# Turning half of each sample's key pages in 32x32 blocks on VectorE, the other half on TensorE, in one core's hybrid decoder layer

## The reference, cut to what matters

```python
q, k, v, g_a, qi, wi, ki, u, g_b = project(hs, ln_g[layer], w_in[layer])
o_a = sample_attention(q, k, v, qi, wi, ki, cache_k[layer], cache_v[layer],
                       cache_idx_k[layer], page_table, rel_bias)
o_b = multiscale_pool(u_full, past - POOL_STATE, POOL_STATE, w_pool[layer], pool_scale[layer])
hs = merge(hs, o_a, g_a, o_b, g_b, w_out[layer])      # x + [o_a*silu(g_a); o_b*silu(g_b)] @ w_out
...
# sparse_attend: logits of each query against the selected keys of its group
logits = jnp.einsum('btgrd,btkgd->btgrk', qg, k_sel, preferred_element_type=F32) * (D ** -0.5)
p = jax.nn.softmax(logits + bias, axis=-1)
o = jnp.einsum('btgrk,btkgd->btgrd', p.astype(v_sel.dtype), v_sel)
```

## Time and profile before

| | us |
|---|---|
| median of three runs | 2083.04 (2082.86 to 2083.18) |
| span of the profiled execution | 2081.8 |
| TensorE busy | 2067.9 (99%) |
| VectorE busy | 1288.9 (62%) |
| ScalarE busy | 735.1 (35%) |
| GpSimd busy | 406.3 (20%) |
| the segment "ga" in the trace | about 1315 to 1615 |

### The profile page before, as it was taken

The page is one execution under the profiler, slowest core; times in us unless marked ns, Lnnn a source line. Parts: engine busy times, 40 slices in busy tenths (PEclk is TensorE's granted clock), DMA queues, the critical chain, the costliest instruction groups (busy, mean ns, idle before and its releaser), DMA issues. The chain is left out here.

```text
span 2081.8 us, 38884 instructions
## 1 busy us (share of the span) xinstructions
PE 2067.9 (99%) x14191; PEld 1973.7 (95%) x14191; DVE 1288.9 (62%) x1747; ACT 735.1 (35%) x917; POOL 406.3 (20%) x574
## 2 busy tenths in 40 slices
PE   9999999999999999999999999999999999999998
PEld 7888888999999999999999999999999999999998
DVE  5545545578687445666776767565565866555664
ACT  6433333322222333333333323333334433333333
POOL 1100000021210010235642103222222511111100
PEclk9999999999999999999999999999999999999999
DMA  8777777755554565665666657878877855555554
GB/s 234 208 220 214 222 211 203 212 167 159 157 160 140 179 192 171 176 195 174 195 201 201 178 153 231 242 245 260 248 248 246 258 170 169 164 164 165 157 167 147
DMA packets 341330, 406.03 MB, mean 195 GB/s; under 512 B 20332, under 2 KB 316204, under 8 KB 341000
## 3 DMA queue, kind: packets, MB, share of 16 engines
q1 hardware_dynamic: 293704, 291.75, 47.6%
q0 software_dynamic: 29968, 94.61, 14.7%
q10 hardware_dynamic: 17584, 18.70, 2.7%
HBM read 377.68 MB, written 31.45 MB: 197 GB/s over the span
## 5 line engine op out<-in xcount | busy, mean ns | idle before, releaser
L246 DVE TENSOR_TENSOR lo<-raw,hi 128x1024 fp32r<-128x1024 f32 x542 | 694.5, 1285 | 566.6 <-ACT hi L241 565.2
L270 PE MATMUL main<-XX,hi 128*128 128x320 f32 x3264 | 1030.1, 316 | 0.2 <-DVE XX L1655 0.2
L272 PE MATMUL main<-XX,lo 128*128 128x320 f32 x3264 | 1009.5, 309 | 0.0
L271 PE MATMUL main<-XX,hi 128*128 128x320 f32 x3264 | 1009.0, 309 | 0.0
L241 ACT ACTIVATE hi<-raw 128x1024 fp32r<-128x1024 f32 x542 | 569.8, 1057 | 854.7 <-PE main L272 540.6
L270 PEld LDWEIGHTS main<-XX,hi 128*128 128x128 f32 x3264 | 613.2, 188 | 9.0 <-issue 5.0
L271 PEld LDWEIGHTS main<-XX,hi 128*128 128x128 f32 x3264 | 613.3, 188 | 2.3
L272 PEld LDWEIGHTS main<-XX,lo 128*128 128x128 f32 x3264 | 612.7, 188 | 0.0
L257 PE MATMUL main<-XX,hi 128*128 128x512 f32 x1024 | 355.9, 392 | 0.0
L258 PE MATMUL main<-XX,lo 128*128 128x256 f32 x1024 | 287.0, 280 | 0.0
L257 PEld LDWEIGHTS main<-XX,hi 128*128 128x128 f32 x1024 | 191.6, 187 | 42.4 <-issue 0.2
(11 more groups left out here) (304 smaller groups left out, 1544.8 us busy)
## 6 DMA issues: line engine op xcount, KB each, us to landing
raw<-w_in SPq DMA_DIRECT2D x416, 512.0 KB, 3.9
raw<-w_out SPq DMA_DIRECT2D x128, 512.0 KB, 3.7
deck<-cache_k POOLq DMA_DIRECT2D x64, 256.0 KB, 4.4
projT<-stg ACTq DMA_DIRECT2D x35, 320.0 KB, 2.9
keep<-cache_v POOLq DMA_DIRECT2D x40, 256.0 KB, 3.4
deck<-cache_v POOLq DMA_DIRECT2D x24, 256.0 KB, 3.6
deck<-maskD POOLq DMA_DIRECT2D x8, 516.0 KB, 5.6
ipg<-cache_idx_k POOLq DMA_DIRECT2D x64, 64.0 KB, 3.1
```

The costliest lines, as they stand in the source:

```text
L246: nc.vector.tensor_tensor(low, raw[:, slot, :, 0:width], high.bitcast(F32), ALU.subtract).then_inc(lo_ready, 1)
L270: nc.tensor.matmul(sums, wh, XH[:, k, :], start=first, stop=False)
L271: nc.tensor.matmul(sums, wh, XL[:, k, :], start=False, stop=False)
L272: mm = nc.tensor.matmul(sums, wl, XH[:, k, :], start=False, stop=last)
```

## The change

TensorE transposes only pages 0 to 3 of a sample, two in s = 1 and two in s = 2, and ScalarE copies all four. Pages 4 to 7 are turned by VectorE straight from `kpg` to `KTs`: 16 instructions a sample, each turning the 32x32 blocks of one row quarter and one column quarter in all four pages and four groups at once. They are spread by two tables. For a sample with u = 0 (after the first) 4 stand in slot 14 and 1 in slot 15 of the quad before, then 4, 4 and 3 in slots 0, 1 and 2. For u = 1 there are 4 in slot 6, 5 in slot 7, none in slot 8, 3 in slot 9 and 4 in slot 10. Sample 0 has 8 in slot 1 and 8 in slot 2. The first turn waits for the sample's pages (e_kw) and for the scores of the sample before (e_s); the last one raises e_kd, for which the scores in s = 3 and the next load of pages 4 to 7 wait. GpSimd loads pages 4 to 7 first, after e_kd, and then pages 0 to 3, after e_kt. VectorE's loop over the quads has its first one written out apart.

```diff
+        e_kw, e_kd = sem("e_kw"), sem("e_kd")
...
+            PE_PAGES = PAGES // 2
...
                 if s in (1, 2):
-                    for p in range(4 * s - 4, 4 * s):
+                    for p in range(2 * s - 2, 2 * s):
                         if p == 0:
-                            pe.wait_ge(e_k, b * (16 * PAGES) + 16 * PAGES)
+                            pe.wait_ge(e_k, b * (16 * PE_PAGES) + 16 * PE_PAGES)
...
-                        if p >= 4:
-                            pe.wait_ge((e_kcA, e_kcD)[p % 2], b * (PAGES // 2) + (p - 4) // 2 + 1)
                         for g in range(G):
-                            tr = nc.tensor.transpose(sbank[p % 4][:, g * P:(g + 1) * P], kpg[:, p, g * P:(g + 1) * P], ident[:])
+                            tr = nc.tensor.transpose(sbank[p][:, g * P:(g + 1) * P], kpg[:, p, g * P:(g + 1) * P], ident[:])
                         tr.then_inc(e_kt, 1)
                 if s == 3:
-                    pe.wait_ge(e_kcA, b * (PAGES // 2) + PAGES // 2)
-                    pe.wait_ge(e_kcD, b * (PAGES // 2) + PAGES // 2)
+                    pe.wait_ge(e_kcA, b * PE_PAGES + PE_PAGES)
+                    pe.wait_ge(e_kd, b + 1)
                     pe.wait_ge(e_kn, b * 2 + 2)
...
-            def turned_keys(eng, copy, s, b, even, done):
-
+            def keys_free(eng, b):
                 eng.wait_ge(e_s, b)
                 eng.wait_ge(w_pe, 4 * NG)
                 eng.wait_ge(ut_out, 16 * NG * (NB_S + 1))
-                for p in range(4 * s - 4 + (0 if even else 1), 4 * s, 2):
-                    eng.wait_ge(e_kt, b * PAGES + (p + 1))
-                    copy(KTs[:, :, p * P:(p + 1) * P], sbank[p % 4].rearrange("p (g n) -> p g n", g=G)).then_inc(done, 1)
+
+            def turned_pages(dve, b, start, count):
+
+                if not count:
+                    return
+                if start == 0:
+                    dve.wait_ge(e_kw, b * (16 * (PAGES - PE_PAGES)) + 16 * (PAGES - PE_PAGES))
+                    keys_free(dve, b)
+                    alone(dve)
+                for i in range(start, start + count):
+                    a, j = i // 4, i % 4
+                    src = kpg[32 * a:32 * a + 32, PE_PAGES:PAGES, :].rearrange("p n (g k) -> p n g k", g=G)
+                    dst = KTs[32 * j:32 * j + 32, :, PE_PAGES * P:PAST].rearrange("p g (n k) -> p n g k", k=P)
+                    ins = nc.vector.transpose(dst[:, :, :, 32 * a:32 * a + 32], src[:, :, :, 32 * j:32 * j + 32])
+                if start + count == 16:
+                    ins.then_inc(e_kd, 1)
+
+            TURNS = ({-2: 4, -1: 1, 0: 4, 1: 4, 2: 3}, {-2: 4, -1: 5, 0: 0, 1: 3, 2: 4})
+            FIRST_TURNS = {1: 8, 2: 8}
...
                 if s in (1, 2):
-                    turned_keys(act, lambda o, i: nc.scalar.activation(o, i, ACT.Copy), s, b, True, e_kcA)
+                    keys_free(act, b)
+                    for p in range(2 * s - 2, 2 * s):
+                        act.wait_ge(e_kt, b * PE_PAGES + (p + 1))
+                        nc.scalar.activation(KTs[:, :, p * P:(p + 1) * P], sbank[p].rearrange("p (g n) -> p g n", g=G),
+                                             ACT.Copy).then_inc(e_kcA, 1)
...
-            def dve_weave(dve, q, j):
+            def dve_weave(dve, q, j, first=False, last=False):
                 u, s = j // 8, j % 8
                 b = q * BQ + u
-                if s in (1, 2):
-                    turned_keys(dve, nc.vector.tensor_copy, s, b, False, e_kcD)
+                if s in (6, 7) and not (last and u):
+                    turns = TURNS[1 - u]
+                    turned_pages(dve, q * BQ + (u + 1), 0 if s == 6 else turns[-2], turns[s - 8])
+                if s in (0, 1, 2):
+                    turns = FIRST_TURNS if first and u == 0 else TURNS[u]
+                    turned_pages(dve, b, sum(n for at_, n in turns.items() if at_ < s), turns[s] if s in turns else 0)
...
-                load_pages(pool, 0, "cache_k", keys, e_k)
+                load_pages(pool, 0, "cache_k", keys, e_k, 0, PE_PAGES)
+                load_pages(pool, 0, "cache_k", keys, e_kw, PE_PAGES)
...
                 with pool.Fori(1, NB_S) as b:
-                    pool.wait_ge(e_kt, b * PAGES)
+                    pool.wait_ge(e_kd, b)
                     alone(pool)
-                    load_pages(pool, b, "cache_k", keys, e_k)
+                    load_pages(pool, b, "cache_k", keys, e_kw, PE_PAGES)
+                    pool.wait_ge(e_kt, b * PE_PAGES)
+                    alone(pool)
+                    load_pages(pool, b, "cache_k", keys, e_k, 0, PE_PAGES)
```

More of the change, by code:

```diff
@@ L422, in hybrid_layer @@
         gated_a, exped_a = sem("gated_a"), sem("exped_a")
-        (e_in, e_rel, e_k, e_v, e_mask, e_masked, e_vnew, e_kt, e_kcA, e_kcD, e_kn, e_s, e_lg, e_mx, e_exp, e_ri, e_pt,
+        (e_in, e_rel, e_k, e_v, e_mask, e_masked, e_vnew, e_kt, e_kcA, e_kn, e_s, e_lg, e_mx, e_exp, e_ri, e_pt,
          e_ptA, e_pv, e_on, e_ot, e_o) = (sem(n) for n in (
-             "e_in", "e_rel", "e_k", "e_v", "e_mask", "e_masked", "e_vnew", "e_kt", "e_kcA", "e_kcD", "e_kn", "e_s", "e_lg",
+             "e_in", "e_rel", "e_k", "e_v", "e_mask", "e_masked", "e_vnew", "e_kt", "e_kcA", "e_kn", "e_s", "e_lg",
              "e_mx", "e_exp", "e_ri", "e_pt", "e_ptA", "e_pv", "e_on", "e_ot", "e_o"))
@@ L1656, in dve_mix, with then_mix @@
                                         ALU.subtract).then_inc(f_lo, 1)
-            def then_mix(weave, mix):
+            def then_mix(weave, mix, **kw):
                 def last_weave(eng, q, j):
-                    weave(eng, q, j)
+                    weave(eng, q, j, **kw)
                     if j in (13, 14):
@@ L1814, in on_gpsimd @@
                     pool.wait_ge(stored[half], 16 * segs["ga"][4])
-                pool.wait_ge(e_kt, NB_S * PAGES)
+                pool.wait_ge(e_kt, NB_S * PE_PAGES)
+                pool.wait_ge(e_kd, NB_S)
                 pool.wait_ge(e_kn, NB_S * 2)
@@ L1870, in on_vector @@
             def on_vector(dve):
-                with dve.Fori(0, NQ - 1) as q:
+                dve_quad(dve, "ga", 0, lambda eng, q, j: dve_weave(eng, q, j, first=True), gate=gate)
+                with dve.Fori(1, NQ - 1) as q:
                     dve_quad(dve, "ga", q, dve_weave, gate=gate)
-                dve_quad(dve, "ga", NQ - 1, then_mix(dve_weave, dve_mix), gate=gate, open_end=True)
+                dve_quad(dve, "ga", NQ - 1, then_mix(dve_weave, dve_mix, last=True), gate=gate, open_end=True)
                 dve_quad(dve, "out", 0, mix_weave(dve_mix, dve_gating), turned=turn_part, first=True)
```

## The result

The changed kernel takes 2117.61 us (median of four runs, 2117.39 to 2118.09) against 2083.09 for the kernel before (median of four as well): a ratio of 1.0166, 95% interval 1.0154 to 1.0178. It is 34.5 us slower. The profiled execution spans 2116.1 us, 34.3 more than before.

What follows compares the result with a forecast made beforehand. TensorE, busy 99% of the span, was taken as the bound. Span 2081.8 - 14.0 (transposes) + 33.6 (stalls) + 3.5 (clock) = 2104.9 us; with the runs' median 1.2 above the span, 2106 us, range 2098 to 2119.

Steps and rivals of the forecast that it cites:

- rival 1: Clock behind TensorE's stalls: falls each time, four chunks at half speed, 14 us in place of 3.5, 2116 us; chance 0.24.
- Gain on TensorE: TensorE's queue before the scores: 16 fewer transposes, 1.75 us less for each of 8 samples, 14.0 us in all.
- Price of a turn: VectorE's 32x512 turn: 0.70 us with the step between instructions, extended from rows of 128, 192 and 256 elements.
- rival 2: VectorE's turns are cheap: at 0.50 us stalls cancel the gain (2083), below it faster; chance 0.10 shared with another rival.
- Stalls: TensorE ahead of the scores: 8.4 us at sample 0, three of 5.0, four of 2.55, together 33.6 us.
- Clock: TensorE's clock behind stalls: one slow chunk, 3.5 us, for the longest stall, nothing for the others; bounds 0 to 14.
- Edits at nothing: Split key loads, turns in slots 6 and 14, late splits and output-stage loads: all covered by slack, costing nothing.
- margin of the loads: Late key pages land some 9 us after the scores begin, VectorE asks later than 11 us: 2 us of margin.
- None hides another: The eight stalls add up, since each chain starts anew at a half quad's evacuation, which waits for TensorE.

Runs made afterwards that it cites:

- filled run: Changed kernel with idle matmuls (56, 34 or 17) put in TensorE's queue ahead of its wait for the turns; 2107.26 us, ratio 1.0116.
- five pages: Changed kernel with sample 0 on TensorE and ScalarE, other turns in VectorE's idle places, and VectorE turning five of eight pages in samples 1 to 7; 2098.69 us.
- sample 0 taken back: Changed kernel, but TensorE transposes all eight pages of sample 0, ScalarE copies them and VectorE turns none; 2108.98 us, ratio 1.0121.

## Why the prediction came out as it did

The direction and the mechanism held: TensorE's queue was the bound, 14.0 us left it, and VectorE's queue behind each evacuation held up the scores eight times (at sample 0 behind the stage's first splits). The measured time, 2117.6 us, lies in the range but at rival 1's 2116, not at the forecast's 2106; the loss was 34.5 us where 23 were forecast. It lies outside the 2098 to 2111 that the prediction gave its own mechanism, and is in the range only because that took in rival 1. That rival 1 comes within 2 us is in part luck: it had 33.6 us of stalls and 14 of clock, the runs show 37.2 and 10.8, and the two misses cancel.

- **Gain on TensorE**, 14.0 us: with 15 of 16 turns left out 13.4 were measured.
- **Price of a turn**, 0.70 us: 702 ns in the row, and (1416.11 - 1413.25) / 4 = 0.715 from turn to turn. The slope through three sizes held, and rival 2 needed 0.50. The prices of the Trainium skill's section on the three transpose paths ("VectorE: DVE Perf Modes"), which are for bf16, did not carry over: VectorE takes 0.70 us for as many elements as a 128x128 tile has, TensorE's transposes step by 0.109 us.
- **Stalls**, 33.6 us: measured 37.2 (8.80, 16.4 at samples 2, 4 and 6, 11.9 at the odd ones). The terms were 8.4, 15.0 and 10.2. What was left out is the step between unlike instructions: from a split to the turn behind it are 1413.25 - 1411.99 = 1.26 us, where the earlier trace rows have (1402.91 - 1400.63) / 2 = 1.14 a split. For samples 2, 4 and 6 three such places and 0.015 more for each of 11 turns make 3 x 0.12 + 0.17 = 0.5 us a sample.
- **Clock**, 3.5 us: this is the step that failed. The prediction charged one chunk for the longest stall and nothing for the rest. The clock fell after all four long stalls and after one of 2.91 us, and cost 10.8 us by the traces and 10.35 by the filled run. The mis-sizing was in how often, not in how much: per stall it was 1.6 to 2.7 us, under the 3.5 charged. For the short stalls the nearest row, 1.5 us at full clock, was what it went by, and three of four bore it out. The three stalls of 5 us were put at nothing without a reason, although nothing between 1.5 and 5 us had been seen; they cost 2.7, 2.5 and 2.4 us, 7.6 of the 10.8. The Trainium skill, "TensorE: Matmul & The Clock Gate", part 1, puts such stalls at risk, and here the trace agrees with it: 0.50 granted behind 5.56 us.
- Sum by the measured terms: - 14.0 + 37.2 + 10.8 = 34.0, against 34.3 between the spans.
- **Edits at nothing** held in the changed kernel: no wait for a key page, none at the normalisation, and VectorE still waits 1.84 us for TensorE at the evacuation in slot 15. The margin of the loads was larger than the 2 us put on it. The last late page of sample 2 is issued at 1386.10, pages land 3.7 us after issue in this stretch, and VectorE's first turn stands at 1396.39:

```profile
1386.10 0.54 POOL L1794 DMA_DIRECT2D deck<-cache_k  x1 [0.69 <-issue]
...
1396.39 2.84 DVE L1471 STREAM_TRANSPOSE deck<-deck 32x512 f32<-32x512 f32 x4
```

That makes some 6 us: VectorE asks 15.1 us after the scores of 1381.28, not 11. The runs with turns in slot 5, and five pages most of all, used the margin up.

- "None hides another" held: without sample 0's stall the others stayed at 28.0 us, where they had 28.4.

## What to carry to other kernels

Mean load says whether work fits on an engine at all; where it fits is read from the instruction that others wait for, back to the last point at which that queue was itself held. Work behind such a point (here the evacuation and the gate) adds to the chain one for one, while the same instructions in places where the engine waits anyway are nearly free (here until the loads of their pages came too late): moving the turns of seven samples took 36 us off, by a table of small numbers. And a stall of TensorE by 3.67 us or more cost more than its length each time here, since what came behind it ran at half clock; so first remove the stalls, and then price the rest.

## What the runs showed of the hardware

**The clock behind a stall.** By the lengths of the scores in the traces (1.97 us at full clock): no stall up to 1.96 us slowed them; of nine of 2.91 to 3.01 us four did (changed kernel one of four, sample 0 taken back two of four, five pages its only one); all twelve of 3.67 to 8.80 us did. So a stall near 3 us goes either way, even between samples of one execution. In the changed kernel each of the five drops cost 1.6 to 2.7 us. These are the idle times in the brackets of the traces, and all of them stand in a stream that otherwise keeps TensorE busy.

**Turns on VectorE in fp32.** 314, 378, 436, 702 and 836 ns for 128, 192, 256, 512 and 640 elements on 32 partitions: 1.04 ns per element from 256 on. The first two sizes read another tile (`main`, a PSUM bank) than the others, so the slope below 256 compares unlike operands. The Trainium skill, "Vector Engine (DVE) Microarchitecture Reference", section 3.8, has the reorder array sustain one element per cycle and lane; a constant price per element is what these rows show too. Consecutive turns don't overlap (702 ns long, 715 apart). Most turns behind a split don't either (split 1.23 us long, turn 1.26 behind its start), but a sample's first turn does, as in slot 14 (1395.25 to 1396.39, 1.14 us), as a copy does in the kernel before (1437.12 to 1438.20, 1.08 us for a split of 1.16). Why the first turn differs stays open.
